# Hybrid attention and expert layer on one core: attention by tile units with gate matmuls between them, and the two differential maps blended by TensorE in the turn, with a diagonal from GpSimd

## The chip, the cores and the metric

The kernel runs on one core of a Trainium2 chip. The metric is the device time of one execution in microseconds (us). Engines: TensorE (PE; its weight loads are PEld), VectorE (DVE), ScalarE (ACT), GpSimd (POOL), SyncE (SP, which here only starts DMAs). TensorE's array runs at 1.2 or 2.4 GHz; the profile shows the granted clock as a share, 0.50 or 1.00 and means between them.

## The reference, cut to what matters

One decoder layer over 1024 tokens of width 1024, in float32. The part that the change touches:

```python
def sliding_window_attention(q, k, v, sinks):    # 8 query heads, 2 key/value heads
    ...
    p = jax.nn.softmax(jnp.concatenate([s, sink_b], axis=-1), axis=-1)[..., :-1]
    o = jnp.einsum('bnhgqk,bnkhd->bnqhgd', p.astype(v.dtype), vc)   # 128 + 128 keys
def diff_attention(q, k, v, lam):                # 4 heads, causal, two maps each
    ...
        p = jax.nn.softmax(jnp.where(causal, s, -jnp.inf), axis=-1)
        a = p[:, :, 0] - lam * p[:, :, 1]
        return jnp.einsum('bhqk,bkhe->bqhe', a.astype(v.dtype), v)
    ...
ob = rms_norm(diff_attention(qb, kb, vb, lam), diff_subln_g[l]) * (1.0 - lam_init)
yb = ob.reshape(B, S, DIFF_V_W) @ w_diff_out[l]
mixed = jax.nn.sigmoid(ga) * ya + jax.nn.sigmoid(gb) * yb    # ga, gb: gates, projected from h
x = x + mixed @ w_o[l]
x = x + moe_ffn(...)                             # 4 of 32 experts
```

## The kernel before, in words

The program has two blocks, `attention_half` and `expert_half`; a barrier stands between them. The change is in the first, and in one wait of the second (`residual`). The first half has these stages, one after the other on PE:

1. RMSNorm, turn of h into `hT` and the projection (L515, L531, L542), up to 279.5 us.
2. The loop over 64 **units** (L568 to L608), up to about 531 us. `UNITS` goes over 8 query tiles `i` of 128 tokens, 4 heads `j`, and the kinds "swa" (sliding window: the heads j and j+4, on the two halves `c` of the array's rows) and "diff" (differential head j, its two maps as `c`). A diff unit has i+1 key tiles, a swa unit 2 (1 at i = 0).
3. The turn of both outputs (L626, L632), up to 547.9 us.
4. Gates and branches: 16 steps m (8 column slabs d by 2 halves of 512 tokens), each with 16 gate calls (L648) and 8 branch calls (L655) of 512 columns, up to 884.4 us. Then the expert block starts with the output projection (L1251).

A float32 matmul call of `pe.matmul` shows in the trace as two MATMUL instructions, each with its own weight load; a `pe.transpose` shows as one.

What sets the order in the loop is written out by hand, on each engine by the loop over u, with semaphores between them:

- **PE**: `scores(u)` (L568; half c waits until the exponentials of unit u-1 have freed its PSUM pair), `product(u-2)` (L604 swa, L608 diff), `turn_p(u-1)` (L582: 128x128 transposes of the probabilities).
- **DVE**: `mix(u-1)`, `maxima(u)`, `store_p(u-1)`, `finish(u-2)`. `maxima` masks and takes row maxima (L407, L409) and forms the negative bias (L414, L417, L419). `mix` takes reciprocals of the sums (L434, L436), forms the blend coefficient (L439) and, for diff, adds the two maps over all keys (L443). `finish` scales the product (L463, L466) and sums its squares (L468).
- **ACT**: `exps(u)` (L283, with L288 for the sinks), then `store_p(u-1)` (L297, PSUM to SBUF).
- **POOL**: nothing in this half. **SP** starts no load between the projection weights and the end of the loop, where it loads the first gate slabs (L220) and the branch weights (L228, L229), then w_o (L232). At the end it loads x again over `hT` with one DMA of 4 MB (L237), after the last gate matmul.

After the loop DVE scales `obn` in two passes per tile (L484, L486) before PE turns it.

In the expert block DVE first splits a bias (`split_bias`, L1034 to L1043), then per token tile t adds x to the projection (L1052) and normalizes; ACT's first norm waits for two small DMAs (L845, L846) that stand behind the router and expert weights on SP's queue.

## Time and profile before

| | us |
|---|---|
| median of 3 runs | 3001.46 (2997.08 to 3006.98) |
| profiled execution | 3002.64 |
| its span | 3000.8 |
| PE busy | 2642.1 (88%) |
| DVE busy | 1481.6 (49%) |
| ACT busy | 364.6 (12%) |
| POOL busy | 724.8 (24%) |
| mean granted clock of TensorE | 0.931 |

The span runs from the first to the last instruction. "Busy" of PE counts a matmul from its start to its modelled end, so rows of short matmuls overlap; how fast they follow each other is read from the start of one group to the start of the next. A mean over the span mixes the two halves; the stages of the first half are read by windows.

### The profile page before, as it was taken

How to read it: one execution, taken by the hardware profiler on the slowest of the kernel's cores; microseconds unless marked ns; L12 is line 12 of the kernel's file. 1: busy time of each engine (PE TensorE's matmuls, PEld its weight loads, DVE VectorE, ACT ScalarE, POOL GpSimd, SP SyncE). 2: the span in 40 equal slices, each digit the busy share in tenths (PEclk: the TensorE clock that was granted, in tenths of full speed). 3: DMA queues.
4: the chain of work that ended last, by engine and by line, in shares of the span. 5: the costliest groups of instructions: out<-in, count | busy, mean ns of one | idle time of the engine just before them, and what ended most of it. 6: DMA issues, size and time to landing. Idle time of an engine off the chain costs nothing.

```text
span 3000.8 us, 63110 instructions
## 1 busy us (share of the span) xinstructions
PE 2642.1 (88%) x22972; PEld 1187.1 (40%) x22973; DVE 1481.6 (49%) x2879; ACT 364.6 (12%) x870; POOL 724.8 (24%) x623
## 2 busy tenths in 40 slices
PE   8999988899998868799999989899889879997755
PEld 4644666444444422244433424234333323332212
DVE  4342787201114445466666656565555546664334
ACT  2001554100001200000000000000000000000002
POOL 0000000000000323244444424244334333442112
PEclk9998798899999879899999989999999999998878
DMA  3100000500025478731556283935786775579993
GB/s 134 56 28 1 1 1 1 154 28 21 21 86 173 143 245 320 255 119 26 191 179 200 71 306 106 363 113 176 258 296 211 242 273 186 189 249 368 378 355 133
DMA packets 166005, 499.22 MB, mean 166 GB/s; under 512 B 46032, under 2 KB 82384, under 8 KB 132944
## 3 DMA queue, kind: packets, MB, share of 16 engines
q1 hardware_dynamic: 108176, 459.96, 40.8%
q0 software_dynamic: 29168, 38.39, 6.7%
q10 hardware_dynamic: 28608, 0.19, 0.5%
q8 instruction: 29, 0.48, 0.1%
q14 instruction: 24, 0.20, 0.0%
HBM read 466.64 MB, written 32.15 MB: 166 GB/s over the span
## 4 chain that ended last, share of the span: by engine, by line
PE 41%; DMA 26%; issue 1%; SPq 1%; DVE 1%; ACT 0%; DVEq 0%; ACTq 0%; POOLq 0%; POOL 0%
PE xbank L1283 24%; DMA w_hi<-in_w 17%; PE xbank L1306 13%; DMA reg_r<-in_w 9%; PE xbank L1251 3%; PE xbank L1293 1%; PE xbank L1300 0%; DVE reg_h L1213 0%; PE xbank L1237 0%; DMA w_hi<-in_b 0%; SPq L868 0%; DMA reg_h<-acc_rows 0%; PE xbank L1224 0%; SPq L877 0%; DMA acc_rows<-stage,idxs 0%
## 5 line engine op out<-in xcount | busy, mean ns | idle before, releaser
L1183 DVE COPY reg_r<-reg_r 128x2048 f32 x580 | 678.5, 1225 | 467.4 <-DMA reg_r<-in_w 219.5
L1283 PE MATMUL xbank<-reg_r,stage 128*32 128x512 f32 x4640 | 572.5, 630 | 102.6 <-DVE reg_r L1183 81.0
L1306 PE MATMUL xbank<-reg_r,stage 128*32 128x256 f32 x9280 | 561.3, 391 | 79.8 <-DMA reg_r<-in_w 79.4
L1283 PE MATMUL xbank<-w_hi,stage 128*32 128x512 f32 x4640 | 555.2, 613 | 58.4 <-DMA w_hi<-in_w 58.3
L1306 PEld LDWEIGHTS xbank<-reg_r,stage 128*32 128x32 f32 x9280 | 312.5, 113 | 318.1 <-DMA reg_r<-in_w 103.4
L933 POOL DMA_INDIRECT acc_rows<-stage,idxs x145 | 340.9, 2351 | 120.9 <-POOL idxs L930 110.0
L1283 PEld LDWEIGHTS xbank<-reg_r,stage 128*32 128x32 f32 x4640 | 157.9, 114 | 427.6 <-issue 277.1
L1283 PEld LDWEIGHTS xbank<-w_hi,stage 128*32 128x32 f32 x4640 | 153.5, 112 | 393.4 <-issue 261.7
L930 POOL TENSOR_TENSOR idxs<-idxa,tok 128x1 int32<-128x1 int32 x145 | 28.8, 199 | 971.1 <-ACT stage L1000 940.0
L531 PE MATMUL pair<-reg_r,reg_h 128*128 128x512 f32 (+1 forms) x640 | 253.2, 551 | 0.3 <-DMA reg_r<-in_w_in 0.3
L923 POOL DMA_INDIRECT stage<-xn_rows,idxg x147 | 192.8, 1311 | 121.5 <-POOL idxg L920 113.0
L994 ACT ACTIVATE stage<-stage 128x256 f32<-128x256 f32 x145 | 60.5, 417 | 1297.5 <-DVE stage L1165 978.2
L905 POOL DMA_DIRECT2D bcs<-order_table x1 | 0.8, 756 | 886.3 <-POOLq L86 886.3
L920 POOL TENSOR_TENSOR idxg<-idxa,tok 128x1 int32<-128x1 int32 x147 | 205.7, 1400 | 14.5 <-DMA idxa<-slot_rows 13.3
L531 PEld LDWEIGHTS pair<-reg_r,reg_h 128*128 128x128 f32 x640 | 119.3, 191 | 114.6 <-issue 110.5
L1190 DVE STREAM_TRANSPOSE stage<-stage 128x256 f32<-128x256 f32 x147 | 63.1, 429 | 183.9 <-DMA stage<-xn_rows,idxg 183.8
L1000 ACT ACTIVATE stage<-xbank,idxa 128x256 f32<-128x256 f32 x145 | 68.4, 472 | 472.6 <-PE xbank L1306 453.2
L1251 PE MATMUL xbank<-reg_r 128*128 128x512 f32 x256 | 114.2, 605 | 9.4 <-DVE reg_h L1052 7.5
L648 PE MATMUL pair<-reg_h,reg_ka 128*128 128x512 f32 x256 | 114.3, 606 | 4.2 <-DMA reg_r<-in_w_diff_out 4.2
L648 PE MATMUL pair<-reg_h,reg_g 128*128 128x512 f32 x256 | 111.2, 592 | 0.0
L1165 DVE TENSOR_SCALAR stage<-xbank 128x256 f32<-128x256 f32 x145 | 61.4, 423 | 70.5 <-PE xbank L1283 70.3
L283 ACT ACTIVATE reg_r<-pair,small 128x256 f32<-128x256 f32 (+7 forms) x128 | 76.8, 600 | 114.4 <-DVE small L417 58.2
(187 smaller groups left out, 1959.8 us busy)
## 6 DMA issues: line engine op xcount, KB each, us to landing
reg_r<-in_w SPq DMA_DIRECT2D x256, 1024.0 KB
w_hi<-in_w SPq DMA_DIRECT2D x128, 1024.0 KB, 5.6
idxa<-slot_rows ACTq DMA_DIRECT2D x596, 0.2 KB
reg_r<-in_w_in SPq DMA_DIRECT2D x4, 2048.0 KB, 7.9
reg_r<-in_x SPq DMA_DIRECT2D x8, 512.0 KB, 3.4
reg_ka<-in_w_in SPq DMA_DIRECT2D x8, 512.0 KB, 3.8
reg_g<-in_w_in SPq DMA_DIRECT2D x8, 512.0 KB, 3.9
reg_r<-in_w_o SPq DMA_DIRECT2D x1, 4096.0 KB, 17.1
```

Of the source, the lines that this page charges most:

```text
L283: act.activation(probs[u % 2][c][:, 0:n], pair[c][:, 0:n], ACT.Exp, bias=nm[:, s:s + 1], scale=ATT_SCALE, accum_out=lsum[:, s:s + 1]).then ...
L531: ins = pe.matmul(bank[n % 2][:, 0:w], hT[:, k, t * P:(t + 1) * P], wv[:, k, :], start=(k == 0), stop=(k == KD - 1))
L648: ins = pe.matmul(bank[br][:, :], wv[:, k, :], hT[:, k, tok], start=(k == 0), stop=(k == KD - 1))
L920: pool.tensor_tensor(idxg[b][:, :], idxa[:, bass.ds(n, 1), 0], group, ALU.add).then_inc(idxg_ready, 1)
L923: pool.indirect_dma_start(out=xg[b], out_offset=None, in_=xn_parts, in_offset=bass.IndirectOffsetOnAxis(ap=idxg[b][:, :].bitcast(U32), axi ...
L933: pool.indirect_dma_start(out=acc_parts, out_offset=bass.IndirectOffsetOnAxis(ap=idxs[b][:, :].bitcast(U32), axis=0), in_=yrow[b], in_offs ...
L1000: act.activation(yrow[b], y_bank[b][:, 0:DG], ACT.Copy, scale=gate_a[:, bass.ds(n, 1), 1]).then_inc(y_taken, 1)
L1183: dve.tensor_copy(w1k[k], lo_from[:, bass.ds(slot, 1), k, :].rearrange("p o n -> p (o n)")).then_inc(w1_filled[k], 1)
L1190: dve.transpose(xT[b], xg[b]).then_inc(xT_ready, 1)
L1251: ins = pe.matmul(bank[2 + half][:, :], mixT[:, k, t * P:(t + 1) * P], wo_s[:, k, half * 512:(half + 1) * 512], start=(k == 0), stop=(k == ...
L1283: ins = pe.matmul(up_bank[b][QB * c:QB * c + QB, :].rearrange("p (h k q) -> p h k q", h=2, q=QB), xT[b][:, QB * k:QB * k + QB], w1k[k].rea ...
L1306: ins = pe.matmul(y_bank[b][QB * j:QB * j + QB, 0:DG], actT[b][:, QB * k:QB * k + QB], w2r[:, k, j * DG:(j + 1) * DG], start=False, stop=( ...
```

## The change

The units become 40: per tile one swa unit with all 8 heads, then four diff units. Between units PE does `fill` matmuls: the gates of branch 0 for the first four slabs (64 of the 256 gate calls), one or two calls per unit by the table `FILLS`; ACT copies each finished group to `mixT`. The turn becomes real matmuls: for diff units the transposed blend p0 + coef * p1 is formed in PSUM from two matmuls per key tile, with the identity and with a diagonal `blend` from POOL; for swa units the diagonal `diag` holds 1/sum. `finish` goes from DVE to ACT. The swa product yields the turned output directly, so that only the diff output is turned at the end, by a diagonal with the RMS scale. x comes back in 8 DMAs with a semaphore each. The pieces of the diff below stand in the order SP, POOL, ACT (`finish`), DVE (`mix`, the scale of `obn`), PE (`turn_p` for swa and for diff, `product`, the loop and what follows it), DVE in the expert block.

```diff
-UNITS = [(kind, i, j) for i in range(NT) for j in range(4) for kind in ("swa", "diff")]
+UNITS = [(kind, i, j) for i in range(NT) for kind, j in [("swa", 0)] + [("diff", j) for j in range(4)]]
+AHEAD = 4
+FILLS = [2] * 15 + [2, 2, 2, 1, 1] * 2 + [2, 2, 1, 1, 1] + [2, 1, 1, 1, 1] + [1, 1, 1, 1, 1]
...
+SLABS = [(d, 0) for d in range(AHEAD)] + [(d, 1) for d in range(AHEAD)] + [(d, br) for d in range(AHEAD, KD) for br in range(2)]
+def gates_of(m):
+    return [1] if m // 2 < AHEAD else [0, 1]
...
             sp.wait_ge(pv_ready, NU)
-            sp.wait_ge(o_taken, NU)
...
-            sp.wait_ge(gate_ready, 4 * KD)
-            sp.dma_start(x2, a["x"][0].rearrange("(t p) n -> p t n", p=P)).then_inc(x_back, 16)
+            sp.wait_ge(gate_ready, gates_before(2 * KD - 1, 1) + 1)
+            for t in range(NT):
+                sp.dma_start(x2[:, t, :], x_d[t]).then_inc(x_back[t], 16)
+        @block.gpsimd
...
+                if kind == "swa":
+                    pool.wait_ge(r_ready, i + 1)
...
+                    for c in range(2):
+                        pool.tensor_tensor(diag[c], ident.unsqueeze(1).to_broadcast([P, 4, P]),
+                                           r8[:, 4 * c:4 * c + 4].unsqueeze(2).to_broadcast([P, 4, P]), ALU.mult).then_inc(diag_ready, 1)
+                else:
+                    pool.wait_ge(mix_ready, u + 1 - units_before("swa", u + 1))
...
+                    pool.tensor_scalar(blend[u % 2], ident, mix_c[:, u % 2:u % 2 + 1], None, ALU.mult).then_inc(blend_ready, 1)
...
+            def finish(u):
...
+                if kind == "swa":
+                    act.activation(qaT[:, :, i * P:(i + 1) * P], bank[6][:, :].rearrange("p (j q) -> p j q", j=4),
+                                   ACT.Copy).then_inc(o_taken, 1)
+                    return
+                act.activation(junk_q, bank[6][:, 0:P], ACT.Square, scale=r, accum_out=ssb[:, 4 * i + j:4 * i + j + 1])
+                act.activation(obn[:, i, j, :], bank[6][:, 0:P], ACT.Copy, scale=r).then_inc(o_taken, 1)
...
-                pr = probs[u % 2]
-                dve.scalar_tensor_tensor(out=pr[0][:, 0:n], in0=pr[1][:, 0:n], scalar=coef[:, 0:1], in1=pr[0][:, 0:n],
-                                         op0=ALU.mult, op1=ALU.add).then_inc(mix_ready, 1)
...
             for i in range(NT):
-                o = obn[:, i, :, :]
-                dve.tensor_tensor(o, o, rstdb[:, 4 * i:4 * i + 4].unsqueeze(2).to_broadcast([P, 4, P]), ALU.mult)
-                dve.drain()
-                dve.tensor_tensor(o, o, subln[:, :].unsqueeze(1).to_broadcast([P, 4, P]), ALU.mult).then_inc(subln_done, 1)
+                dve.tensor_tensor(diag[i % 2], ident.unsqueeze(1).to_broadcast([P, 4, P]),
+                                  rstdb[:, 4 * i:4 * i + 4].unsqueeze(2).to_broadcast([P, 4, P]), ALU.mult).then_inc(scale_ready, 1)
...
+                if kind == "swa":
+                    for c in range(2):
+                        pe.wait_ge(diag_ready, 2 * i + c + 1)
+                        if c:
+
+                            pe.wait_ge(pT_act, low_turns(u) + 1)
+                            if i:
+                                pe.wait_ge(pT_dve, high_turns(u) + 1)
+                        for m in range(n):
+                            for h in range(4):
+                                ins = pe.matmul(bank[4 + m][:, h * P:(h + 1) * P],
+                                                probs[u % 2][c][:, (h * n + m) * P:(h * n + m + 1) * P], diag[c][:, h, :],
+                                                start=True, stop=True)
...
+                pe.wait_ge(blend_ready, u + 1 - units_before("swa", u + 1))
+                for m in range(n):
+                    for c in range(2):
+                        ins = pe.matmul(bank[4 + m // 4][:, (m % 4) * P:(m % 4 + 1) * P], probs[u % 2][c][:, m * P:(m + 1) * P],
+                                        blend[u % 2] if c else ident, start=(c == 0), stop=(c == 1))
...
+                if u >= 1:
+                    pe.wait_ge(o_taken, u)
...
             for u in range(NU + 2):
...
+                if u < NU:
+                    fill(sum(FILLS[:u]), FILLS[u])
+            gates(0)
+            pe.wait_ge(o_taken, NU)
             for i in range(NT):
+                pe.wait_ge(scale_ready, i + 1)
...
+                    ins = pe.matmul(bank[4 + i % 2][:, j * P:(j + 1) * P], obn[:, i, j, :], diag[i % 2][:, j, :], start=True, stop=True)
...
+            gates(1)
...
             for m in range(2 * KD):
+                if m + 2 < 2 * KD:
+                    gates(m + 2)
+                branches(m)
...
-                if t == 0:
-                    dve.wait_ge(x_back, 16)
+                dve.wait_ge(x_back[t], 16)
```

How the order moves. First PE in the loop at tile 1, before: a swa and a diff unit of one head (`reg_ka`/`reg_qa` are swa keys and queries, `reg_qb` diff queries, `tabs_s` the identity, `reg_r` on the right of L582 the probabilities). Rows count calls.

```order
L568 MATMUL pair<-reg_ka,reg_qa 128x256 x2
L604 MATMUL bank<-reg_ka,reg_r 128x64 x4
L582 MATMUL bank<-tabs_s,reg_r 128x128 x2
L568 MATMUL pair<-reg_r,reg_qb 128x256 x2
L608 MATMUL bank<-reg_r 128x128 x2
L582 MATMUL bank<-tabs_s,reg_r 128x128 x4
```

The same place now: the swa unit of tile 1 (L649, turned at L681, product L707), with fills (L725) after each unit and a blend pair (L689, twice) per key tile.

```order
L649 MATMUL pair<-reg_ka,reg_qa 128x256 x8
L711 MATMUL bank<-reg_r 128x128
L689 MATMUL bank<-tabs_s,reg_r 128x128
L689 MATMUL bank<-early,reg_r 128x128
L725 MATMUL bank<-reg_h,reg_g 128x512 x2
L660 MATMUL pair<-reg_r,reg_qb 128x256 x2
L711 MATMUL bank<-reg_r 128x128
L681 MATMUL bank<-early,reg_r 128x128 x16
L725 MATMUL bank<-reg_h,reg_g 128x512 x2
L660 MATMUL pair<-reg_r,reg_qb 128x256 x2
L707 MATMUL bank<-early,reg_ka 64x512 x4
```

Four swa units with 8 score calls, 16 transposes and 16 products of 64 columns have become one with 8, 16 and 4 calls, the products 512 columns wide.

Second, PE behind the last product, before:

```order
L608 MATMUL bank<-reg_r 128x128 x8
L626 MATMUL pair<-tabs_s,reg_r 128x128 x4
L632 MATMUL pair<-tabs_s,reg_r 128x128 x4
...
L648 MATMUL pair<-reg_h,reg_ka 128x512 x16
L655 MATMUL pair<-reg_qa,reg_r 128x512 x4
```

and now:

```order
L711 MATMUL bank<-reg_r 128x128 x8
L738 MATMUL pair<-reg_h,reg_ka 128x512 x8
L770 MATMUL bank<-early,reg_r 128x128 x32
L738 MATMUL bank<-reg_h,reg_ka 128x512 x8
L738 MATMUL pair<-reg_h,reg_ka 128x512 x8
L749 MATMUL pair<-reg_qa,reg_r 128x512 x4
```

Eight gate calls stand before the turn of the outputs and sixteen behind it, ahead of the first use of the branch weights.

Third, POOL, which had no row in this half before, now:

```order
L295 TENSOR_TENSOR early<-tabs_s,small 128x512 x2
L303 TENSOR_SCALAR early<-tabs_s,small 128x128 x4
L295 TENSOR_TENSOR early<-tabs_s,small 128x512 x2
L303 TENSOR_SCALAR early<-tabs_s,small 128x128 x4
```

Two diagonals of 512 columns per tile and one of 128 per diff unit, each of which a turn on PE waits for.

## Rows read from the trace of the kernel before

**Rows 1.** Windows over the first half: busy per engine, granted clock, DMA share, GB/s

```profile
279.00:311.00 32.00, 29.33 (x106) 21.43 (x106) 23.91 (x135) 16.10 (x70) 0.00 (x0) 0.53 0.00 1
375.00:450.00 75.00, 67.19 (x379) 47.67 (x380) 60.74 (x243) 42.34 (x120) 0.00 (x0) 1.00 0.00 1
500.00:531.00 31.00, 25.54 (x122) 19.07 (x121) 17.55 (x56) 11.51 (x26) 0.00 (x0) 0.73 0.01 2
```

**Rows 2.** Waits inside the loop, 279 to 531 us: total, times, longest

```profile
ACT reg_r L283 <- DVE small L417: 58.2, 52, 5.0
PEld pair L568 <- ACT reg_r L283: 46.2, 87, 2.0
```

**Rows 3.** Groups of PE by form, 279 to 531 us: busy, mean ns

```profile
L582 PE MATMUL bank<-tabs_s,reg_r 128*128 128x128 f32 x264 | 48.3, 315 | 0.4 <-DVE reg_r L443 0.3
L608 PE MATMUL bank<-reg_r 128*128 128x128 f32 x288 | 45.8, 310 | 0.8 <-issue 0.8
```

**Rows 4.** Timeline of PE at tile 5: start, length, instructions

```profile
421.75 1.60 PE L608 MATMUL bank<-reg_r 128*128 128x128 f32 x12
423.20 0.60 PE L582 MATMUL bank<-tabs_s,reg_r 128*128 128x128 f32 x4
...
424.81 0.70 PE L568 MATMUL pair<-reg_ka,reg_qa 64*128 64x256 f32 x2 [0.39 <-ACT reg_r L283]
425.44 1.10 PE L604 MATMUL bank<-reg_ka,reg_r 128*128 128x64 f32 x8
```

**Rows 5.** Timeline of PE: first scores of the loop; scores of tile 7 at clock 0.50

```profile
279.51 0.49 PE L568 MATMUL pair<-reg_ka,reg_qa 64*128 64x128 f32 x4 [0.88 <-DVE reg_r L344]
...
502.78 3.79 PE L568 MATMUL pair<-reg_r,reg_qb 64*128 64x512 f32 x8
```

**Rows 6.** Groups of DVE by form, 279 to 531 us

```profile
L407 DVE CUSTOM_DVE_ANT_0 pair<-pair,tabs_s 128x256 f32<-128x256 f32 x56 | 23.8, 424 | 0.5 <-PE pair L568 0.3
L409 DVE TENSOR_REDUCE small<-pair 128x1 f32<-128x896 f32 x8 | 8.7, 1086 | 0.0
L443 DVE SCALAR_TENSOR_TENSOR reg_r<-reg_r,small 128x1024 f32<-128x1024 f32 x4 | 5.1, 1284 | 0.3
```

**Rows 7.** Groups of ACT by form, 270 to 560 us

```profile
L283 ACT ACTIVATE reg_r<-pair,small 128x256 f32<-128x256 f32 x64 | 30.3, 473 | 51.9 <-DVE small L414 46.8 <-DVE small L417 4.6
L297 ACT ACTIVATE reg_r<-bank 128x512 f32<-128x512 f32 x48 | 28.2, 587 | 3.7 <-PE bank L582 3.6
L283 ACT ACTIVATION_READ_ACCUMULATOR reg_r<-pair,small 128x1 f32 x128 | 24.7, 193 | 0.0
```

**Rows 8.** Timeline from the end of the loop to the gates

```profile
531.17 0.66 PE L626 MATMUL pair<-tabs_s,reg_r 128*128 128x128 f32 x4 [0.86 <-DVE small L468]
...
551.46 17.05 PE L648 MATMUL pair<-reg_h,reg_ka 128*128 128x512 f32 x32 [4.18 <-DMA reg_r<-in_w_diff_out]
...
575.22 13.90 PE L648 MATMUL pair<-reg_h,reg_ka 128*128 128x512 f32 x32
```

**Rows 9.** Groups of POOL by form over the whole span; DVE's product of diagonal size

```profile
L920 POOL TENSOR_TENSOR idxg<-idxa,tok 128x1 int32<-128x1 int32 x147 | 205.7, 1400 | 14.5 <-DMA idxa<-slot_rows 13.3 <-issue 0.3
L930 POOL TENSOR_TENSOR idxs<-idxa,tok 128x1 int32<-128x1 int32 x145 | 28.8, 199 | 971.1 <-ACT stage L1000 940.0 <-DMA acc_rows<-stage,idxs 31.1
L484 DVE TENSOR_TENSOR reg_r<-reg_r,small 128x512 f32<-128x512 f32 x8 | 5.5, 684 | 0.1
```

**Rows 10.** Timeline at the start of the expert block

```profile
883.79 0.59 PE L655 MATMUL bank<-reg_qb,reg_r 128*128 128x512 f32 x1
886.26 13.97 PE L1251 MATMUL xbank<-reg_r 128*128 128x512 f32 x32 [1.88 <-PEq L86]
907.75 16.41 PE L1251 MATMUL xbank<-reg_r 128*128 128x512 f32 x32 [7.51 <-DVE reg_h L1052]
916.81 1.06 ACT L963 ACTIVATE stage<-reg_h 128x1024 f32<-128x1024 f32 x1 [38.57 <-DMA acc_rows<-stage]
921.56 0.68 DVE L1052 TENSOR_TENSOR reg_h<-reg_h,xbank 128x512 f32<-128x512 f32 x1
```

More of the change, by code:

```diff
@@ L298, in _, with take_fill @@
+            def take_fill(g):
+                d, half = divmod(g, 2)
+                act.wait_ge(fill_done, g + 1)
+                act.activation(mixT[:, d, half * 512:(half + 1) * 512], bank[7], ACT.Copy).then_inc(fill_taken, 1)
             act.wait_ge(late_in, N_LATE)
-            for u in range(NU + 1):
+            filled = [sum(FILLS[:u]) // KD for u in range(NU + 1)]
+            for u in range(NU + 2):
+                if 1 <= u <= NU and filled[u] > filled[u - 1]:
+                    take_fill(filled[u - 1])
@@ L311, in _ @@
[L311 to L317 removed]
+                act.wait_ge(o_turned, i + 1)
+                act.activation(qbT[:, :, i * P:(i + 1) * P], bank[4 + i % 2].rearrange("p (j q) -> p j q", j=4),
+                               ACT.Copy, scale=sub_c).then_inc(obT_ready, 1)
@@ new lines, in _ @@
+            for m in range(2 * KD):
+                d, half = m // 2, m % 2
+                for br in range(2):
+                    if br in gates_of(m):
+                        act.wait_ge(gate_ready, gates_before(m, br) + 1)
+                        src = gate_bank(m, br)
+                    else:
+                        act.wait_ge(fill_taken, m + 1)
+                        src = mixT[:, d, half * 512:(half + 1) * 512]
+                    if m >= 2:
+                        act.wait_ge(mix_done, m - 1)
+                    act.activation(sg[m % 2][br], src, ACT.Sigmoid,
+                                   bias=gate_bias[:, 8 * br + d:8 * br + d + 1]).then_inc(gate_sig, 1)
@@ L476, in _ @@
                     store_p(u - 1)
-                if u >= 2:
-                    finish(u - 2)
             dve.wait_ge(subln_rms, 1)
@@ L573, in turn_p @@
                 n = len(keys_of(UNITS[u]))
[L574 removed]
                 if u >= 1:
[L576 to L588 removed]
+                    pe.wait_ge(pT_act, low_turns(u))
@@ L592, in product @@
                 keys = keys_of(UNITS[u])
[L593 to L605 removed]
+                pe.wait_ge(pT_act, low_turns(u + 1))
@@ new lines, in product @@
+                if high_turns(u + 1):
+                    pe.wait_ge(pT_dve, high_turns(u + 1))
+                if u >= 1:
+                    pe.wait_ge(o_taken, u)
+                if kind == "swa":
+                    for m, kt in enumerate(keys):
+                        for c in range(2):
+                            ins = pe.matmul(bank[6][64 * c:64 * c + 64, :], va[:, kt, c * HD:(c + 1) * HD],
+                                            pT_s[c][:, m * 512:(m + 1) * 512], start=(m == 0), stop=(m == len(keys) - 1))
@@ new lines, in gates @@
+            def gates(m):
+                d, half = m // 2, m % 2
+                for br in gates_of(m):
+                    slot, use = SLOT_OF[SLABS.index((d, br))]
+                    pe.wait_ge(gw_in[slot], 16 * use)
+                    if m >= 2:
+                        pe.wait_ge(gate_sig, 2 * (m - 2) + br + 1)
+                    for k in range(KD):
+                        ins = pe.matmul(gate_bank(m, br), ring[slot].rearrange("p (k n) -> p k n", k=KD)[:, k, :],
+                                        hT[:, k, half * 512:(half + 1) * 512], start=(k == 0), stop=(k == KD - 1))
+                    ins.then_inc(gate_ready, 1)
@@ new lines, in branches @@
+            def branches(m):
+                d, half = m // 2, m % 2
+                for br in range(2):
+                    if m >= 2:
+                        pe.wait_ge(mix_done, m - 1)
+                    oT = (qaT, qbT)[br]
+                    for j in range(4):
+                        ins = pe.matmul(bank[2 + br + 2 * (m % 2)], w_sd[:, br, j, d * P:(d + 1) * P],
+                                        oT[:, j, half * 512:(half + 1) * 512], start=(j == 0), stop=(j == 3))
+                    ins.then_inc(y_ready, 1)
```

324 lines of the change are left out of this document (166 added, 158 removed).

## The prediction

> **What bounds the kernel now.** I read the windows first, then the waits, then the timeline. The expert half is touched only through its start, so what counts is the stretch from 279.5 us (first scores, [rows 5]) to the last branch matmul at 884.4 us [rows 10]. It has three parts.
>
> (a) The loop with the turn behind it, 279.5 to 551.5 us: 272.0 us. PE is shown busy nearly throughout [rows 1], but that is not work: the instructions are short and each is drawn with its latency. At full clock a product instruction of 128 columns follows the last after 0.12 us (12 in the 1.45 us from 421.75 to 423.20), though it is drawn 0.31 us long [rows 3, 4]. The loop is a chain: scores, row maxima on DVE, exponentials on ACT, next scores. ACT waited 58.2 us for one of DVE's bias steps alone, and PE's weight loads 46.2 us for the exponentials [rows 2]. The clock is part of it: 0.53 over the first tile and 0.73 over the last, 1.00 over 375 to 450 us [rows 1].
>
> (b) Of these, 531.2 to 551.5 us are the turn of the outputs and a wait for the branch weights, whose loads start only when the loop is over; after it the first 32 gate instructions take 17.05 us instead of 13.90, since the clock has to come back [rows 8].
>
> (c) Gates and branches, 551.5 to 884.4 us, 332.9 us: 384 calls of 512 columns, two instructions each at 0.429 us (32 in 13.90 us [rows 8]), 0.858 us a call, 329.5 us, and 3.2 for the slow start. PE never waits there. A gate call moved into PE's real idle time of the loop is a saving.
>
> **The change, part by part.** Everything at full clock first.
>
> *PE work in the new loop.* Turn of diff units: 144 key tiles (4 heads by 36), two calls each, so 4 instructions where one transpose stood; at 0.12 us 69.1 us, where 144 transposes cost about 17. Diff products unchanged, 288 by 0.12: 34.6. Swa turn: 120 calls, 240 instructions (16, then 7 by 32): 28.8. Diff scores: the two maps use two halves of the array's rows, and where both are free to go they run side by side: 8 instructions of 512 columns took 3.79 us at clock 0.50, where one after the other they would take 6.9, and the first four of 128 took 0.49 [rows 5]. So 0.214 us per key tile, 144 times: 30.8. Swa scores, 8 calls of 256 columns that alternate between the halves: 16 by 0.214 / 2, 1.7 us a tile, 12.8 in all. Swa products, 4 calls of 512 columns on two halves of the columns: 1.7 a tile, 12.8; that halves of the columns overlap as halves of the rows do is my assumption, bounded by +12.8. Fills: 64 by 0.858, 54.9. Each unit changes twice between half and whole array; in [rows 4] two score instructions take 0.63 us to the next product where 0.43 would be their columns, so 0.15 to 0.2, 80 times: 12. Sum 256 us.
>
> *Is PE then the pace?* For a diff unit of n key tiles PE needs 0.93n + 0.3 + 0.86 per fill: 2.9 us at tile 0, 4.8 at tile 2, 8.6 at tile 7. The other chain at tile 7, from exponentials to exponentials: `mix` 0.6, two maxima of 1.5 (1.09 for the 896 columns [rows 6], the masked part and the bias), one exponential about 1.3: 5.2 us. DVE no longer has the sum of the maps (1.28 us for 1024 columns [rows 6]) or `finish`. At tile 0 the chain is about 2.3 us. So PE paces diff units everywhere. ACT gets `finish` (two short ones, 0.7 us with the read of the sum, at 0.19 [rows 7]), the swa exponentials and a copy per 8 fills (0.59 [rows 7]); in sum 2.3 us at tile 0 and 4.2 at tile 7 of 2.9 and 8.6, covered. If PE were faster there, ACT at tiles 0 and 1 would be late next. PE's `product(u)` now waits for `finish(u-1)` because there is one result bank; behind it stand the turn and the fills. ACT does that `finish` right after the copy, some 3.1 us after the scores, as PE arrives (2.9 + scores 0.3), so nothing at this precision.
>
> *The waits that stay.* A swa unit is one long link: after its scores DVE does four maxima a half (0.42 each and the read between, about 2.1 us with the bias [rows 6]), 4.2 for both, then ACT four exponentials of the second half at 0.56 (0.47 and the read, overlapped [rows 7]), 2.25; with releases 7.0 us. PE has meanwhile product and turn of the last diff units (0.72 us per key tile of the tile before), two fills (1.7) and 0.15. At tile 1 it waits 4.4, 0.7 less with each tile, 1.0 at tile 7: 17 us, and 3.5 at tile 0. Then the turn of its second half waits for the copies of the first (0.3 + 0.69 + 0.1, one bank a copy): 1.1 by 7, 8. And it waits for the diagonals of POOL. No POOL operation on 512 columns is in the trace: its rows are of one element a partition, 0.20 and 1.40 us; DVE's product of the same size takes 0.684 [rows 9]. From 0.2 to 2.1 (1.40 and 0.684); I take 1.2, nearest to DVE's row, and 0.5 for the 128 columns of `blend` (0.2 to 1.6). At 1.2 the first diagonal is 2.1 us after the exponentials; product and scores hide that from tile 4 on; 3.5 us in all. With 1.5 for the last unit's copies: waits 34 us.
>
> The page GPSIMD Engine Reference (section 4.1, Engine selection) of the Trainium skill speaks against the place: elementwise work with two inputs is about 2x slower than on VectorE. By that a diagonal takes 1.4 us and the sum grows by 1.5 us; the trace has nothing of that size on POOL to agree or differ.
>
> *Clock.* PE idles 2 to 3 us at the first swa units. Today's loop, with transposes in every unit, was at 1.00 for 75 us and at 0.53 at its thin start [rows 1]; the new one is denser. I add 5 us of lost clock, between nothing (as in 375 to 450) and 25 (half the first three tiles at 0.50). The loop: 256 + 34 + 5 = 295 us.
>
> The page TensorE: Matmul & The Clock Gate (Part 4) of the Trainium skill says that transposes do not count as activity for the clock. If so, with every transpose of the loop a matmul now, the 5 us would be nearer 0; the 75 us at 1.00 show that they do not bring it down alone.
>
> *Behind the loop.* Eight gate calls (6.9 us) cover the last `finish`, the root with its table load, the reciprocal and the first diagonal, about 4.2 us. Turn of one output: 8 tiles of 8 instructions, 0.96 us, and ACT's copy 0.6 beside them: 9.5 us with its ends. The branch weights, 4 MB, still start at the loop's end, but have 6.9 + 9.5 + 13.7 us of PE work before their first use; today they take 20 us behind the turn and with gate slabs between. Hidden; without that cover a few us. The rest is 320 calls by 0.858, 274.5 us. New stretch: 295 + 274.5 + 9.5 = 579.0 against 604.9: 25.9 us less.
>
> *Start of the expert block.* Today PE waits 7.5 us for the first residual, which stands behind the bias split, whose input waited behind the 4 MB of x on the DMA rings; then it runs slow (16.41) [rows 10]. Now x is requested two steps (20 us) earlier, and the bias lands some 7 us sooner. But ACT's first norm starts at 916.81, 30.5 us after the block's start, behind two small DMAs that SP issues after router and expert weights, and the residual of tile 1 follows it at 921.56 [rows 10]. That does not move: PE would wait there instead. So of 9 us I count 1 (0 to 9).
>
> Sum: 3002.6 - 25.9 - 1.0 = 2975.7 for the profiled execution, which lies 1.2 above the median of the three runs: **2975 us**.
>
> **The rivals.**
> - *Less waiting* (0.17): maxima and exponentials of swa units overlap better, the clock never falls, the block start gives more. 5 + 6 + 4 us less: 2960.
> - *POOL late* (0.12): operations at 2.1 and 1.6 us. Each blend of tiles 0 and 1 comes about 1 us late (8 us) and each swa turn 0.9 (6): 2989. For it speaks the row of 1.40 us; against it that of 0.20 [rows 9].
> - *The clock stays low in the loop* (0.10, the other side). The waits at the swa units bring it to 0.50, and then PE, which now paces, pays every one. At the 0.83 that the loop's windows average today, 256 us of work grow by 52, of which about 20 go into waits that were there: 32 more, 3007. It decides when the loss passes 27 + 5 us, a mean clock under about 0.84. For it: 0.53 and 0.73 [rows 1]. Against: these stretches had less work per us.
> - *Halves do not run side by side* (0.05): 56 us more, 3031. [Rows 5] speak against it.
>
> **How the numbers follow.** Forecast 0.56. A measurement of this kernel can tell about 0.3%, 9 us, from no change. Faster by more: forecast, less waiting, and most of POOL late: 0.82. Slower by more (over 3010): half of the low clock, and the halves: 0.09. Within: 0.09. The range takes in less waiting with the full 9 us of the block start, and POOL late with 6 us of lost clock: 2950 to 2996.
>
> **What would show it.** Right: the loop is 285 to 305 us long; granted clock there above 0.93; PE's waits in it are few and long, for the exponentials of swa units (up to 5 us, once a tile); no wait for the branch weights; blend turns do not wait for POOL from tile 2 on; the projection of token tile 2 starts at most 2 us earlier relative to its block. Wrong: a loop over 315 us, a wait at every blend, or a second load stage that PE waits for between gates. The first steps to fail would be the 0.12 us of a turn instruction (816 of them on turns, so 0.01 us is 8 us) and the 7.0 us link.

## The result and the profile after

The changed kernel takes 2955.18 us (median of 4 runs, 2952.99 to 2962.66), the kernel before 3000.49 on the same chip: ratio 0.9845, 95% interval 0.9826 to 0.9864. It is faster, inside the range of 2950 to 2996, but by 45 us where 26 were forecast. The profiled execution took 2956.45 us, its span is 2954.5.

Windows of the changed kernel, in the columns of [rows 1]; the first is the whole loop:

```profile
279.10:564.60 285.50, 268.48 (x1612) 185.01 (x1613) 123.61 (x518) 133.70 (x422) 35.67 (x48) 0.96 0.04 12
279.10:311.00 31.90, 25.95 (x116) 14.56 (x116) 12.64 (x80) 14.25 (x62) 4.46 (x6) 0.89 0.00 1
311.00:378.00 67.00, 62.19 (x302) 39.05 (x302) 26.52 (x131) 31.33 (x115) 9.44 (x13) 0.90 0.06 16
378.00:564.60 186.60, 180.34 (x1194) 131.39 (x1195) 84.45 (x308) 88.12 (x248) 21.76 (x30) 1.00 0.05 13
```

The loop is 34 us longer than before (285.5 against 251.5), yet the profile shows TensorE idle in it for only 17.0 us, for 24.9 before. VectorE's busy time fell from 187.5 us in the loop before to 123.6. The granted clock is 1.00 from 378 us on.

Waits inside that loop (total, times, longest), answering to [rows 2]:

```profile
PE pair L660 <- ACT reg_r L353: 6.8, 7, 1.3
PE bank L681 <- DVE early L558: 4.4, 5, 0.9
PE bank L681 <- ACT early L370: 3.5, 3, 1.4
PE bank L681 <- POOL early L295: 1.2, 1, 1.2
PEld pair L660 <- ACT reg_r L353: 12.9, 9, 2.2
```

Groups by form in the loop, answering to [rows 3, 9]: the two halves of the blended turn, the product, and GpSimd's two operations.

```profile
L689 PE MATMUL bank<-tabs_s,reg_r 128*128 128x128 f32 x288 | 56.5, 278 | 0.0
L689 PE MATMUL bank<-early,reg_r 128*128 128x128 f32 x288 | 55.7, 275 | 0.0
...
L303 POOL TENSOR_SCALAR early<-tabs_s,small 128x128 f32<-128x128 f32 x32 | 19.4, 605 | 180.7 <-DVE small L549 180.6
...
L295 POOL TENSOR_TENSOR early<-tabs_s,small 128x512 f32<-128x512 f32 x16 | 16.3, 1041 | 340.5 <-DVE small L539 340.5
```

Timeline of TensorE, first at the sliding-window unit of tile 1, then at a differential unit of tile 7:

```profile
309.71 0.70 PE L660 MATMUL pair<-reg_r,reg_qb 64*128 64x256 f32 x2 [1.35 <-ACT reg_r L353]
311.54 1.22 PE L660 MATMUL pair<-reg_r,reg_qb 64*128 64x256 f32 x2 [1.13 <-ACT reg_r L353]
...
313.33 3.75 PE L681 MATMUL bank<-early,reg_r 128*128 128x128 f32 x16
317.95 2.02 PE L681 MATMUL bank<-early,reg_r 128*128 128x128 f32 x16 [0.87 <-DVE early L558]
...
539.64 1.99 PE L660 MATMUL pair<-reg_r,reg_qb 64*128 64x512 f32 x8
541.57 2.05 PE L711 MATMUL bank<-reg_r 128*128 128x128 f32 x16
543.45 0.39 PE L689 MATMUL bank<-tabs_s,reg_r 128*128 128x128 f32 x2
543.68 0.39 PE L689 MATMUL bank<-early,reg_r 128*128 128x128 f32 x2
...
547.03 1.02 PE L725 MATMUL bank<-reg_h,reg_g 128*128 128x512 f32 x2
547.98 1.99 PE L660 MATMUL pair<-reg_r,reg_qb 64*128 64x512 f32 x8
```

In this differential unit of tile 7 nothing waits: scores, product, 32 turn instructions in 3.58 us, one gate matmul, 8.34 us a unit. At tile 1 the exponentials are late twice, and 16 turn instructions take 3.75 us at 313.33 and another 16 of the same form 2.02 at 317.95: the first lot ran right after the waits at the lower clock (0.50, 1.2 GHz, over 313.33 to 317 us; 1.00 behind 317.95).

Behind the loop and at the start of the expert block, answering to [rows 8, 10]:

```profile
564.64 7.03 PE L738 MATMUL pair<-reg_h,reg_ka 128*128 128x512 f32 x16
571.51 7.95 PE L770 MATMUL bank<-early,reg_r 128*128 128x128 f32 x64
579.30 7.03 PE L738 MATMUL bank<-reg_h,reg_ka 128*128 128x512 f32 x16
...
849.15 13.97 PE L1372 MATMUL xbank<-reg_r 128*128 128x512 f32 x32 [1.89 <-PEq L112]
869.76 16.05 PE L1372 MATMUL xbank<-reg_r 128*128 128x512 f32 x32 [6.64 <-DVE reg_h L1173]
886.53 13.90 PE L1372 MATMUL xbank<-reg_r 128*128 128x512 f32 x32
...
859.25 1.22 DVE L1156 CAST b1p<-w_hi 96x2048 bf16<-96x2048 f32 x1 [8.93 <-DMA w_hi<-in_b]
877.25 1.06 ACT L1085 ACTIVATE stage<-reg_h 128x1024 f32<-128x1024 f32 x1 [40.80 <-DMA acc_rows<-stage]
```

No wait for the branch weights and no slow first gates. From the loop's start to the last branch matmul, which ends at 847.3, it is 568.1 us against 604.9: 36.8 less. The block's start to its third projection went from 38.6 to 37.4 us. The expert matmuls start at 1029.99 against 1069.64, 39.7 us sooner; the remaining 6.7 us lie in the expert part, whose code is the same. From its first matmul to the end of the span it took 1924.5 us here and 1931.2 before, and between 1920.0 and 1939.1 in the profiles of all kernels of this study. So this part tells nothing of the change, and below each experiment is read by its loop and its block start in one profile, with the median beside it.

### The profile page after: what moved, and what is told of

The parts are those of the page before. It is cut to its first block, busy times and chain, and to the rows that moved or that the text cites. A ratio compares the mean times of both kernels' runs of the same rounds, so it can differ in the third digit from the quotient of the medians.

```text
span 2954.5 us, 63506 instructions
## 1 busy us (share of the span) xinstructions
PE 2626.8 (89%) x23344; PEld 1180.6 (40%) x23345; DVE 1408.3 (48%) x2597; ACT 371.4 (13%) x910; POOL 754.5 (26%) x671
## 4 chain that ended last, share of the span: by engine, by line
PE 42%; DMA 25%; issue 1%; DVE 1%; SPq 1%; ACT 0%; DVEq 0%; ACTq 0%; POOLq 0%; POOL 0%
PE xbank L1404 24%; DMA w_hi<-in_w 17%; PE xbank L1427 13%; DMA reg_r<-in_w 8%; PE xbank L1372 3%; PE xbank L1414 1%; PE xbank L1358 1%; PE xbank L1421 0%; DVE reg_h L1334 0%; DMA w_hi<-in_b 0%; SPq L990 0%; DMA reg_h<-acc_rows 0%; PE xbank L1345 0%; SPq L999 0%; DMA acc_rows<-stage,idxs 0%
## 5 line engine op out<-in xcount | busy, mean ns | idle before, releaser
L1404 PE MATMUL xbank<-reg_r,stage 128*32 128x512 f32 x4640 | 579.7, 636 | 101.5 <-DVE reg_r L1304 80.2
L1427 PEld LDWEIGHTS xbank<-reg_r,stage 128*32 128x32 f32 x9280 | 306.5, 112 | 316.3 <-DMA reg_r<-in_w 104.5
L1055 POOL DMA_INDIRECT acc_rows<-stage,idxs x145 | 331.1, 2284 | 121.2 <-POOL idxs L1052 116.9
L1404 PEld LDWEIGHTS xbank<-reg_r,stage 128*32 128x32 f32 x4640 | 157.5, 115 | 434.9 <-issue 285.9
L295 POOL TENSOR_TENSOR early<-tabs_s,small 128x512 f32<-128x512 f32 x16 | 16.3, 1041 | 340.5 <-DVE small L539 340.5
L1372 PEld LDWEIGHTS xbank<-reg_r 128*128 128x128 f32 x256 | 48.8, 193 | 68.8 <-issue 61.3
L1281 DVE TENSOR_SCALAR sel<-e_all,fcs 96x32 bf16 (+1 forms) x146 | 34.5, 237 | 82.7 <-PE xbank L1427 82.6
```

The costliest lines, as they stand in the source:

```text
L1055: pool.indirect_dma_start(out=acc_parts, out_offset=bass.IndirectOffsetOnAxis(ap=idxs[b][:, :].bitcast(U32), axis=0), in_=yrow[b], in_offs ...
L1372: ins = pe.matmul(bank[2 + half][:, :], mixT[:, k, t * P:(t + 1) * P], wo_s[:, k, half * 512:(half + 1) * 512], start=(k == 0), stop=(k == ...
L1404: ins = pe.matmul(up_bank[b][QB * c:QB * c + QB, :].rearrange("p (h k q) -> p h k q", h=2, q=QB), xT[b][:, QB * k:QB * k + QB], w1k[k].rea ...
L1427: ins = pe.matmul(y_bank[b][QB * j:QB * j + QB, 0:DG], actT[b][:, QB * k:QB * k + QB], w2r[:, k, j * DG:(j + 1) * DG], start=False, stop=( ...
```

## The experiments

The loops in one table, each from its first scores to the first gate call behind it (windows of each profile). "Idle" is the length less TensorE's busy time. The time is the median; the kernel before lay between 3000 and 3008 beside each. The kernels e4 and e7 have the changed kernel's loop, and theirs took 285.5 and 286.7 us: differences of about 1 us are scatter.

| kernel | loop us | PE busy | idle | clock | time us | ratio to before |
|---|---|---|---|---|---|---|
| changed | 285.5 | 268.5 | 17.0 | 0.96 | 2955.2 | 0.9845 |
| e1_no_fills | 254.2 | 225.7 | 28.5 | 0.93 | 2983.5 | 0.9929 |
| e2_dve_blend | 260.5 | 235.9 | 24.6 | 0.93 | 2939.2 | 0.9767 |
| e2b_dve_blend_mm | 261.0 | 241.8 | 19.2 | 0.96 | 2940.1 | 0.9774 |
| e3_dve_diag | 288.7 | 270.1 | 18.6 | 0.96 | 2965.0 | 0.9860 |
| e5_pool_twice | 296.1 | 273.3 | 22.8 | 0.95 | 2976.3 (one run) | not taken |
| e8_all | 260.4 | 235.8 | 24.6 | 0.93 | 2928.7 | 0.9744 |
| e9_refill | 244.1 | 226.3 | 17.8 | 0.98 | 2906.9 | 0.9669 |
| e10_refill_mm | 248.5 | 235.8 | 12.7 | 0.98 | 2915.2 | 0.9707 |
| e11_refill_alone | 272.6 | 260.1 | 12.5 | 0.98 | 2950.8 | 0.9821 |

### The gate matmuls out of the loop: e1_no_fills

```diff
-AHEAD = 4
-FILLS = [2] * 15 + [2, 2, 2, 1, 1] * 2 + ...
+AHEAD = 0
+FILLS = [0] * 40
```

All 384 gate and branch calls now stand behind the loop. The gate slabs are loaded in the new order.

> The changed kernel without any gate matmul in the loop: all 256 gate calls come after it, in the same two-steps-ahead order. Theory A (PE paces the new loop, so a fill is only free in the waits of the swa units and in the units of tiles 0 to 2, where the chain over DVE and ACT is longer than PE's bare work): the loop, 285.5 us in the changed kernel, shrinks by about 34 us, the gates behind it grow by 54.9, the sum is 21 us slower than the changed kernel, about 2976 us. Rival B (the chain over DVE and ACT paces the loop and the fills lie in its shadow): the loop shrinks by less than 10 us and the kernel lands at 3000 to 3010 us.

Measured: 2983.5 us, 0.9929 (0.9901 to 0.9958). The loop is 31.3 us shorter and the expert block starts at 873.20, 24.1 later than in the changed kernel, where theory A had 21. 64 calls at 0.858 us are 54.9 us behind the loop; in the loop they cost 31. The gate matmuls between the units bring 24 us of the 37, the rest of the change the other 13. Without them the loop, 254.2 us, is no shorter than the 251.7 us (279.51 to 531.17) of the kernel before: those 13 us come from behind the loop, where the turn of the outputs and the wait for the branch weights took 20.3 us and the turn now takes 7.8, and where the slow first gates (17.05 us for 13.90) are gone. Of the 24 us that the gate matmuls bring, 11.5 are idle time (28.5 to 17.0), and the rest is busy time that the clock and waits drawn as busy had lengthened (42.8 us more for 54.9 us of work).

### The blend back on VectorE: e2_dve_blend and e2b_dve_blend_mm

```diff
-                    for c in range(2):
-                        ins = pe.matmul(bank[4 + m // 4][...], probs[u % 2][c][:, m * P:(m + 1) * P],
-                                        blend[u % 2] if c else ident, start=(c == 0), stop=(c == 1))
+                    ins = pe.transpose(bank[4 + m // 4][...], probs[u % 2][0][:, m * P:(m + 1) * P], ident)
```

VectorE's `scalar_tensor_tensor` blends the maps first, as before the change, and GpSimd's `blend` goes. In e2b the last line is a matmul with `ident` instead.

> The changed kernel with the blend of the two differential maps back on DVE, and the diff turn by one transpose per key tile instead of four matmul instructions. Theory A (PE paces): 432 instructions at 0.112 us, 48 us, leave PE; the units are then set by the chain with the blend in it (about 2.75 us at tile 0, 3.95 at tile 2, 6.6 at tile 7, where the changed kernel has 8.3), the swa waits grow by some 10 us: the loop shrinks by about 22 us, the kernel lands at about 2933 us, faster than the change. Rival C (taking the blend off DVE is where the gain comes from): the loop grows by 10 us or more, 2965 us or more. If transposes do not keep the clock up, the granted clock of the loop falls below 0.9 and takes 10 us or more of A's gain.

Measured: 2939.2 us, 0.9767 (0.9736 to 0.9798), loop 25.0 us shorter, expert block at 823.83, 25.3 sooner. Theory A. In the changed kernel a tile-7 unit takes 8.34 us, here 6.09 (522.17 to 528.26). The second part of the change, the blend on TensorE, costs 25 us beside the form it replaced; only the gate matmuls, the shorter turn of the outputs and the removed stall make the whole a gain. That GpSimd's `blend` goes too is not the cause: e3, below, takes it away as well and gains nothing.

> VectorE blends the maps as in the kernel before, and the turn of a differential map is one matmul with ident per tile (two instructions each, as every fp32 matmul here) in place of one transpose. It separates what the turn's form costs from what the blend's place costs: the one-transpose form gave 2939.2, the changed kernel 2955.2. Theory A (TensorE paces the loop and every instruction of a turn is worth 0.111 us in it): 144 more instructions than the one-transpose form = +16 us, of which the waits for the exps that form still has (about 40 us by the trace) take some back: loop 266 to 272 us against 260.4 and 285.5, time 2945 to 2951. Rival B (the transposes cost by their effect on the clock, so that matmuls win it back): time 2939 or less, loop 260 or less, a granted clock nearer 1.00 in the tiles 1 and 2. Rival C (instruction count does not matter where the chain of VectorE and ScalarE paces): within 2 us of 2939.

Measured: 2940.1 us, 0.9774 (0.9741 to 0.9807): the time of e2. 144 more instructions, 16 us at 0.111, and a loop 0.5 us longer. The next 288 instructions, from here to the changed kernel, are 32 us and make it 24.5 us longer. Idle time fell by 5.4 us, and busy time rose by 5.9 only. The other 10 us of work are covered in two ways. One is the clock, 0.96 over the loop for 0.93. Windows around the sliding-window unit of tile 7, of e2_dve_blend:

```profile
501.00:504.00 3.00, 2.84 (x5) 0.81 (x4) 1.77 (x6) 2.10 (x8) 2.02 (x2) 0.68 0.00 0
504.00:508.00 4.00, 4.00 (x17) 3.56 (x17) 1.52 (x4) 1.82 (x4) 0.01 (x1) 0.50 0.01 4
```

and of e2b_dve_blend_mm:

```profile
501.00:504.00 3.00, 3.00 (x8) 1.03 (x7) 1.28 (x6) 2.79 (x13) 0.01 (x1) 1.00 0.01 3
504.00:508.00 4.00, 4.00 (x28) 3.00 (x27) 2.84 (x8) 2.69 (x6) 2.03 (x2) 1.00 0.02 4
```

In e2 TensorE waited 0.5 us each before 493.34 and 499.24, for exponentials, and then worked at its lower level for some 7 us (0.53 in 502 to 503, 0.50 to 508, 0.55 in 508 to 509); in e2b, where longer turns fill those two waits, the clock stays at 1.00, although the eight scores at 501.45 take 3.93 us, which hides a wait of another 2. The other way are waits that the busy time hides: the scores of the second map wait for their bank while those of the first are drawn, so that the two halves run one after the other. Eight score instructions of tile 7 take 2.71 and 2.45 us in e2 (519.53, 525.88) at full clock, 1.99 in e2b and in the changed kernel. So of the three theories C comes nearest, with B's clock as a part of it: as long as VectorE's and ScalarE's chain is the longer one, the instructions are nearly free.

The page TensorE: Matmul & The Clock Gate (Part 4) of the Trainium skill says that transposes do not count as activity for the clock, which would be rival B. These two runs do not decide it, since waits and transposes differ together; and e9_refill, below, has transposes in each differential turn and a clock of 1.00 from 311 to 378 and from 450 to 531 us. The falls read here stand behind waits, in either form.

### GpSimd's part: e3_dve_diag and e5_pool_twice

e3 makes all diagonals on VectorE, e5 has GpSimd make each of them twice. The edit of e5 for the sliding-window diagonals (that for `blend` is alike):

```diff
+                        pool.tensor_tensor(diag[c], ident..., r8..., ALU.mult)
+                        pool.drain()
                         pool.tensor_tensor(diag[c], ident..., r8..., ALU.mult).then_inc(diag_ready, 1)
```

> The changed kernel with both kinds of diagonals made by DVE instead of GpSimd. Theory A (PE paces, and the diagonals are ready before PE asks, except at the first swa unit): within 4 us of 2955. Rival D (GpSimd's time is on the path of every turn): faster by 8 us or more, since a blend diagonal takes DVE about 0.25 us where GpSimd takes 0.605, and a swa diagonal 0.69 where GpSimd takes 1.04.

Measured: 2965.0 us, 0.9860 (0.9832 to 0.9887); loop 3.2 us longer, expert block 3.2 later. The median is 10 us above the changed kernel's, outside theory A's 4, but the kernel before was 8 us slower beside it, and the ratios differ by less than their intervals. As theory A had it, there is nothing to gain by taking the diagonals from GpSimd.

> The changed kernel with each GpSimd diagonal made twice, one after the other. Theory A: only swa turns of the first tiles see it, 1 us each, the loop grows by 2 to 5 us. Rival D: every blend comes 0.6 us later and every swa diagonal 1 to 2 us, and PE waits for all of it: the loop grows by 25 us or more.

Measured in one run: 2976.3 us, loop 10.6 us longer, block 10.6 later, between the theories. Waits of its turn in the loop, and a window:

```profile
PE bank L686 <- POOL early L298: 6.4, 5, 2.4
```

```profile
300.00:378.00 78.00, 68.88 (x325) 43.59 (x323) 27.45 (x139) 33.51 (x123) 20.27 (x28) 0.87 0.03 8
```

The waits for GpSimd went from 1.2 to 6.4 us, all of them at sliding-window turns; differential turns had one wait of 0.3. Idle time rose by 5.8 and busy time by 4.8, in part since the clock in 300 to 378 us fell from 0.91 to 0.87. In this one run 5.2 us of added waits cost twice their length.

### The expert block's start: e4_zero_first and e7_split_zero

```diff
+            sp.wait_ge(setup, 2)
+            sp.dma_start(xn_d[S:ROWS, :], ...)   # and acc_d, from behind the router weights
             sp.dma_start(g2_b, ...)
...
-            dve.wait_ge(bias_in, 6 * 16)
-            split_bias(b1_all, b1_left, b1p)
             for t in range(NT + 4):
...
                     residual(t)
+                if t == 0:
+                    dve.wait_ge(bias_in, 6 * 16)
+                    split_bias(b1_all, b1_left, b1p)
```

e4 has the first part, e7 both.

> The changed kernel, with the zero rows of the expert block written before its gains and router weights are loaded. In the changed kernel the first norm's ScalarE operation waits for those rows until +28.1 us of the block, but the third projection starts right behind the second, and the second is held by VectorE's bias split. Theory A (the bias split binds first): the first norm moves from +28.1 to about +16 to +20, the second projection stays at +20.6 and the third at +37.4, time within 2 us of the changed kernel's. Theory B (the zero rows bind): the third projection starts 5 us or more sooner relative to the block's start.

Measured in one run: 2956.5 us. The first norm moves from +28.1 to +20.5 us of the block's start, the second projection stays at +19.9 (+20.6 before), the third at +37.0. Theory A: the bias split binds, not the zero rows.

> The changed kernel with both: zero rows first, and VectorE's split of the first biases moved from before the first residual to behind it. Theory A (the second projection waits for the split, then the third for the second): second projection at about +14 to +15 of the block's start instead of +20.6, third at +29 to +32 instead of +37.4, everything behind it 6 us sooner, time 2949. Theory B (something else of the block's start, such as the second token tile's own loads, takes its place): third projection still at +35 or later, time 2953 to 2957.

Measured: 2955.5 us, 0.9834 (0.9804 to 0.9863). The timeline of the block:

```profile
851.34 27.70 PE L1373 MATMUL xbank<-reg_r 128*128 128x512 f32 x64 [1.89 <-PEq L112]
878.88 1.04 PE L1346 MATMUL xbank<-tabs_s,stage 128*128 128x128 f32 x8
879.75 13.90 PE L1373 MATMUL xbank<-reg_r 128*128 128x512 f32 x32
```

The second projection follows the first without a gap, and the third starts at +28.4 instead of +37.4. From the block's start to the first expert matmul it is 174.9 us, against 180.8 in the changed kernel and 183.0 to 185.5 in the seven others that keep the split where it was. In place, then, theory A, with 9 us at the third projection and 6 by the first expert matmul, where 6 were expected. The median, 2955.5, lies where theory B had it: in this profile the block began 2.2 us later and the expert part took 3.7 us more than in the changed kernel's, which uses the 6 us up, and the ratio's interval is 18 us wide. In e8_all the same block again took 173.9 us.

### The best version: e8_all, e9_refill, e10_refill_mm, e11_refill_alone

e8 is e2 with both moves of e7. e9 adds another placing of the same 64 gate matmuls:

```diff
-FILLS = [2] * 15 + [2, 2, 2, 1, 1] * 2 + [2, 2, 1, 1, 1] + [2, 1, 1, 1, 1] + [1, 1, 1, 1, 1]
+FILLS = [2] * 5 + [6, 2, 2, 2, 2] + [6, 1, 1, 1, 1] + [5, 1, 1, 1, 1] + [3, 1, 1, 1, 1] + [2, 1, 1, 1, 1] + [2, 1, 0, 1, 0] + [1, 0, 0, 0, 3]
```

e10 is e9 with the turn of e2b; e11 is the changed kernel with only this line replaced.

> The version that should beat both kernels: VectorE blends and one transpose turns, with the gate matmuls between the units kept, and the two moves at the expert block's start. If the two gains add: the one-transpose form's 2939.2 less 6 = 2933 (ratio to the kernel before about 0.975). If the block's start moves give nothing: 2939.

Measured: 2928.7 us, 0.9744 (0.9719 to 0.9769). The gains add: loop as e2's, third projection at +28.4.

> e8_all (VectorE blends, one transpose turns, the two moves at the expert block's start; 2928.7) with the same 64 gate matmuls of the loop placed otherwise: 6, 6, 5, 3, 2 and 2 of them behind the sliding-window units of token tiles 1 to 6, where TensorE still waits for ScalarE's exps of that unit (1.7 and 1.1 us in tile 1, 1.4 and 0.9 in tile 2, 1.0 and 0.7 in tile 3), fewer behind the differential ones, 3 at the end. Theory A (the fills behind the differential units lengthen them, since TensorE has no wait there, and those waits can be filled): loop 6 to 9 us shorter than 260.3, time about 2922. Theory B (the waits return behind the differential units, whose chain of VectorE and ScalarE then paces): loop within 3 us of 260, time 2926 to 2931.

Measured: 2906.9 us, 0.9669 (0.9630 to 0.9708). The loop is 16.3 us shorter, twice what theory A had. The waits of tile 1 and the turn behind them, in e8_all:

```profile
308.85 0.70 PE L655 MATMUL pair<-reg_r,reg_qb 64*128 64x256 f32 x2 [1.68 <-ACT reg_r L346]
310.67 0.70 PE L655 MATMUL pair<-reg_r,reg_qb 64*128 64x256 f32 x2 [1.12 <-ACT reg_r L346]
...
312.45 3.17 PE L676 MATMUL bank<-early,reg_r 128*128 128x128 f32 x16
```

In e9_refill the same place reads

```profile
304.99 5.32 PE L718 MATMUL bank<-reg_h,reg_g 128*128 128x512 f32 x12
310.23 0.84 PE L655 MATMUL pair<-reg_r,reg_qb 64*128 64x256 f32 x4
...
312.16 2.02 PE L676 MATMUL bank<-early,reg_r 128*128 128x128 f32 x16 [0.36 <-POOL early L295]
```

Six gate matmuls (12 instructions) stand where 2.8 us of waits were, and the clock stays up behind them: in 300 to 378 us it is 1.00 against e8's 0.89. Of the 16.3 us, 6.8 are idle time and 9.5 busy time. (As elsewhere, busy time shrinks by the clock and by waits drawn as busy.)

> e9_refill with each transpose of the turn written as a matmul with ident. In e8_all (transposes) the granted clock is 0.89 in the stretch 500 to 531 us and 0.97 in 375 to 450; with matmuls in their place it was 1.00 in both, TensorE was busy 4.9 us more and the loop took the same time. Expected if that holds here: clock 1.00 there, and a loop within 3 us of e9_refill's; a loop over 5 us longer would say that the 144 instructions (16 us) are given back by the waits, not by the clock.

Measured: 2915.2 us, 0.9707 (0.9667 to 0.9746), an interval that overlaps e9's. The loop is 4.4 us longer, between the two values expected. The clock is 1.00 in 500 to 531 and in 375 to 450 us, as expected, but over the loop it is 0.98 in both, so here it gives nothing back; of the 16 us of instructions 5.1 went into idle time and 6 to 7 into the waits that busy time hides: eight scores of tile 7 take 3.48 and 3.31 us in e9 (502.35, 508.61), 3.05 and 2.40 in e10. TensorE's weight loads of e9 show such a wait, inside a row that PE draws as busy:

```profile
503.85 0.29 PEld L655 LDWEIGHTS pair<-reg_r,reg_qb 64*128 64x128 f32 x2 [0.35 <-ACT reg_r L351]
```

> The changed kernel as it is (GpSimd diagonals, blend on TensorE), with only the placing of the 64 gate matmuls of e9_refill. In e9_refill that placing took the loop from 260.3 to 244.0 us. Theory A (it fills the waits for the exps of the sliding-window units, and with them goes the half clock behind them, in either form): the changed kernel has such waits of 1.4 and 1.1 us in tile 1, 0.7 and 0.9 in tile 2, and a clock of 0.90 to 0.92 between 300 and 378 us, less than the one-transpose form has, so it gains less: loop 274 to 279 us instead of 285.5, time 2944 to 2949. Rival B (it is the room left behind the differential units by VectorE's blend that the placing uses; with the blend on TensorE there is none): loop within 3 us of 285.5, time 2952 to 2958.

Measured: 2950.8 us, 0.9821 (0.9775 to 0.9867); loop 12.9 us shorter, expert block at 837.17, 12.0 sooner. Theory A, and more than it expected: idle time fell by 4.5 us, busy time by 8.3, at a clock of 1.00 in 300 to 378 us where the changed kernel had 0.91. Windows of e11, of the first tile and of that stretch:

```profile
279.00:311.00 32.00, 27.40 (x118) 15.65 (x118) 13.04 (x79) 12.40 (x54) 4.45 (x6) 0.84 0.00 1
300.00:378.00 78.00, 74.66 (x403) 45.98 (x402) 34.95 (x172) 40.74 (x151) 12.13 (x16) 1.00 0.05 14
```

The median is only 4 us lower and the intervals of the two ratios overlap, so the time alone does not show the gain. The profiled execution was the slowest of the four (2962.0 us) and had the longest expert part of all (1939.1 us).

## Why the prediction was right, and where it was off

**The sum for the profiled execution** was 2975.7, measured 2956.5: 19.2 too high. By place, from the spans: loop -9.5 (285.5 for 295), turn of the outputs -1.7 (7.8 for 9.5), gates and branches +0.3 (274.8 for 274.5), start of the expert block -0.2 (1.2 gained for 1), the rest of that block -1.3, an earlier start of the loop -0.3, the expert part -6.7, which is its scatter and no term of the change. The first two of these last three may be scatter as well: the block of the same code took 183.3 us to its first expert matmul in e4 and 183.7 in e11, where the changed kernel's took 180.8. So about 11 of the 19 us are the change's. The direction, the places and the mechanism held; the loop's terms were mis-sized, in part against each other.

**The waits that stay: 34 us forecast, 17.0 measured.** This is the term that failed, and in it the waits for exponentials of sliding-window units: 20.5 us forecast (17 and 3.5 at tile 0), 6.8 shown. The 7.0 us link of a sliding-window unit was the sum of VectorE's two halves and ScalarE's second half. In the trace ScalarE begins with the first half as VectorE begins the second (307.61):

```profile
307.73 0.47 ACT L353 ACTIVATE reg_r<-pair,small 128x256 f32<-128x256 f32 x1 [4.06 <-DVE small L513]
```

Its eight exponentials run on without a gap, 0.45 us each; TensorE gets its second score bank at 311.54, 5.8 us after the scores' end. And each half lets TensorE issue half its scores. So the wait of tile 1 is 2.5 us for 4.4, that of tile 2 1.6 for 3.7, that of tile 3 0.7 for 3.0, and from tile 4 on the profile shows none. Some of the link may still be waited for inside rows drawn as busy: the weight loads of these scores show nine such waits where the matmuls show seven. The second halves of turns waited as reckoned, 7.9 us in all for 8: 0.88 at tiles 1 to 5, 1.43 and 1.33 at tiles 6 and 7 (before 488.31 and 528.41), 0.78 at tile 0. GpSimd: 3.5 forecast, 1.2 measured.

**The clock: 5 us forecast, about 9 measured.** 0.11 of 26.0 busy us to 311, 0.10 of 62.2 to 378 us, nothing behind. e11 bears it out in part: with the waits filled, busy time fell by 8.3 us, of which by the same reckoning (0.16 of 27.4 to 311, nothing behind) some 5 are the clock's, and the rest are waits that were drawn as busy. That the rival "the clock stays low" did not come: the loss behind 378 us is zero, as [rows 1] had for the dense middle of the loop before.

**The work at full clock: 256 us forecast, 268.5 less 9 = 259.5 measured**, with the waits drawn as busy in it. That the two are so near is luck, since the errors cancel. A turn instruction follows the last after 0.111 us (pairs every 0.22 to 0.23, from 543.45), not 0.12: 816 of them, 7 us less. This was named as a step that could fail. Against it, scores of 512 columns take 0.24 us a key tile for 0.214 (8 in 1.93 us), 4 us more in all, sliding-window scores and products 1.9 us a tile for 1.7, 3 more, and what is left, 3.5 us, lies in the pieces between the units and the hidden waits; no run parts the two. Sliding-window products, 8 of 512 columns in 1.87 us (322.26 to 324.13), do overlap by halves of the columns, as assumed; one after the other they would take 3.4.

**GpSimd.** 1.04 us for 512 columns and 0.605 for 128, where 1.2 and 0.5 were taken. By the page GPSIMD Engine Reference (section 4.1) of the Trainium skill, which has two-input work about 2x slower than on VectorE, the estimate was 1.4; the row says 1.04, 1.5 times VectorE's 0.684 [rows 9], and the row decides. The rival POOL late did not come, and e5 shows what it would have been: at twice the durations 10.6 us, and not at the blends but at the sliding-window turns.

**Gates under the loop.** 320 calls by 0.858 us held to 0.3 us, and nothing waited for weights. That gate calls in the loop fill idle time is shown by e1: 54.9 us of work for 31 us of loop.

**The expert block.** The gain of 1 us was right, and by luck, since its reason held only in part. The bias did not land 7 us sooner: the split starts +10.1 us into the block, +11.0 before, though x is requested earlier. What was said to hold the third projection, the zero rows, did not hold it: e4 moved them by 7.6 us and the projection by 0.4. The split held the second projection, and the third followed that. e7 took both away for 9 us. The split moved alone was not run; in the changed kernel the residual of tile 1 starts at 882.00, behind the first norm, so that an estimate from that row has the third projection at about +33.6 of the block, behind the zero rows, and over half of the gain gone. That the two waits end so near each other was read rightly; which would be first in the changed kernel was not.

**What the prediction did not ask** is whether the second half of the change, the blend on TensorE, pays for itself. Its own terms held the answer: 69.1 us of turns where 17 stood, in a loop that it found TensorE to pace. e2 gives the price, 25 us, less than 52 because the turn instructions took 0.111 us (48 us in place of 52) and the chain of VectorE and ScalarE then binds again in part: idle time is 24.6 for 17.0, the clock 0.93 for 0.96, and scores wait inside their own rows.

## What to carry to other kernels

When filler work is put under a chain, TensorE comes to pace the loop, and then work moved to it to relieve another engine is paid for: here the first 16 us of turn instructions cost 0.5 us, the next 32 us cost 24.5. Price each part of such a change against the new bound, not the old one. Put fillers where the waits are rather than evenly: the same 64 matmuls were worth 13 us more in the changed kernel and 16 in the best version, and over half of that was busy time, which shrank as the clock stayed up and as hidden waits went. Where two waits end within a few us, take both away before judging either.

## What the runs showed of the chip

- The work behind a wait pays for it: 16 turn instructions took 3.75 us behind waits of 1.35 and 1.13 us, and 2.02 us later or with the waits filled. Waits of 5.2 us for GpSimd (e5, one run) came with a loop 10.6 us longer, and 4.5 us of idle time less (e11) with one 12.9 shorter.
- Two maps' scores on the two halves of the array's rows take 1.99 us for 8 instructions where both banks are free, and 3.48 where the second comes late (502.35 in e9, at a clock of 1.00). The profile draws all of these 3.48 us as busy.
- GpSimd's product of 128 x 512 fp32 took 1041 ns and its scaling of 128 x 128 605 ns, beside 684 ns on VectorE for the first.
- The expert part, the same in all kernels, took between 1920.0 and 1939.1 us in thirteen profiles, so a gain of under 10 us ahead of it is seen in a timeline and not in a median.
